# Gate projection of the first attention cut into pieces between its units

## The chip, the cores and the metric

The kernel runs on one core of one Trainium2 chip. The metric is the device time of one execution in microseconds (us), the median of several runs. The engines of the core are TensorE (PE, matrix multiplications and transposes), VectorE (DVE), ScalarE (ACT), GpSimd (POOL) and SyncE (SP, which here issues the loads of weights).

## What is computed

Two blocks over a sequence of 256 tokens with 1024 channels, all in float32. The first block has a gated mixer and then a windowed attention; the second has a retention mixer, a latent attention and, twice, a retrieval of experts. The change lies in the windowed attention of the first block. Its reference, cut to what matters:

```python
def swa_mixer(h, k_band, v_band, pos, w_in, b_q, sinks, w_out):
    z = h @ w_in
    q, g = jnp.split(z, 2, axis=-1)
    q = rotary((q + b_q).reshape(...), pos)
    scores = jnp.einsum('bnqhrd,bnkhd->bnhrqk', q, k_band) * (HEAD_DIM ** -0.5)
    scores = jnp.where(mask, scores, -jnp.inf)
    m = jnp.maximum(jnp.max(scores, axis=-1, keepdims=True), sink)
    p = jnp.exp(scores - m)
    p = p / (jnp.sum(p, axis=-1, keepdims=True) + jnp.exp(sink - m))
    o = jnp.einsum('bnhrqk,bnkhd->bnqhrd', p, v_band).reshape(b, s, B_WIDTH)
    y = o * jax.nn.silu(g)
    return y @ w_out
```

16 query heads of 64 channels share 2 key heads; queries come in two blocks of 128. The gate g isn't used before the product with V is there: it only multiplies o.

## The kernel before

**Weights.** All weights stream from HBM in slabs of 128 partitions by 2048 numbers, in one order for the whole kernel (`SLAB_STAGES`). A slab goes through a ring of two places (`ring`, loaded by SP in halves of 1024, L384). ACT rounds each half to the shorter format `w_hi` (`split_half`, L940), and POOL makes the remainder `w_lo` = ring - `w_hi` (L2010). There are four half places for each of `w_hi` and `w_lo`. A load waits until the remainder of the half that stood in its ring place is made (`split_ready`), and a rounding waits until TensorE has used the half that stood in its place (`half_done`). Every product with weights is three matmuls, hi by hi, hi by lo, lo by hi (`triple`, L433 to L435).

**Slabs of the attention.** `b_q` (4 slabs), `b_kv` (1), `b_g` (4, the gate), `b_out` (4). A gate slab has 8 chunks of the contraction and two halves of 128 output channels: 8 x 2 x 3 = 48 matmuls over 256 tokens, into one PSUM bank (`G`), which ACT empties with Silu into `B_gT` (L1033).

**Order on TensorE.** After `b_kv` all four gate slabs are multiplied (`project_cols("b_g", ...)`), then the keys (L648) and the queries (L575) are transposed; ACT and DVE copy these out. Then `attention("b", ...)` runs. It has 12 units: units 0 to 3 hold four heads each of the first query block, units 4 to 11 two heads each of the second. The order is written out by `attention_order`: "s" is a unit's scores (a mask by the identity, L664, then the products, L667), "t" the four transposes of its probabilities (L610), "v" a product with V for one query block and half of the heads (L685). Scores run three units ahead of transposes. Before, the four "v" come after the transposes of units 2, 4, 8 and 11 (`PV_AFTER`), and all share the four banks `X` in turn: a tile waits until the tile four places earlier has been read.

**The other engines in a unit.** DVE takes the maximum (`maximum`, L1460 to L1466), ACT the exponentials (L1070, L1074), DVE divides by the sum (`normalize`, L1474 to L1477), TensorE transposes, ACT copies the transposed probabilities (L1080). On DVE the order is `normalize(k)`, `maximum(k + 2)`, and at a "v" `b_gated`: the product with the gate and its splitting into `B_yh` and `B_yl` (L1643, L1417, L1418).

**After it.** `project_wide("b_out", ...)` multiplies by the output weights: two groups of two slabs, 96 matmuls over 512 columns in all. It began when all four `b_gated` were done. Then the norm of the block and the retention follow.

Of the kernel before, what the change touches and what calls it, by code (L numbers as in the profile page):

```python
# [19 lines left out]
P = 128  # L20
T = 256
NB = T // P
D = 1024
DC = D // P
W_A = 2048
RING = 2
# [7 lines left out]
HEADS_B, KVH, DH = 16, 2, 64  # L34
# [15 lines left out]


UNITS = {"b": 12, "m": 8}
PV_AFTER = {"b": [1, 3, 7, 11], "m": [1, 3, 5, 7]}
AHEAD = 3


def attention_order(name):
    n, out, values = UNITS[name], [], 0
    for k in range(min(AHEAD, n)):
        out.append(("s", k))  # L60
    for k in range(n):
        out.append(("t", k))
        while values < len(PV_AFTER[name]) and (PV_AFTER[name][values] < k or k == n - 1):
            out.append(("v", values))
            values += 1
        if k + AHEAD < n:
            out.append(("s", k + AHEAD))
    return out
# [26 lines left out]
SLAB0, N_SLABS = first_index(SLAB_STAGES)  # L95
# [37 lines left out]
def build(nc, h_kept, slabs, x_in, cols_in, rows_in, ws_in, keys_in, pos_row, pos_col, rope_in, diff_in, out):  # L133
# [4 lines left out]
    with ctx:  # L138
# [269 lines left out]
        def _(pe):  # L408
# [37 lines left out]
                                      c == 0, c == 4 * WIDE[stage] - 1)  # L446
                return last

            def project_wide(stage, src, ready=None, first=0):

                per, groups = WIDE[stage], SLABS[stage] // WIDE[stage]

                def inputs_ready(g, p, half):
                    half_ready(SLAB0[stage] + g * per + p, 0, half)
                    if ready is not None:
                        pe.wait_ge(ready, 2 * p + half + 1)

                for g in range(first, groups):
                    for b in range(NB):
                        bank_free(wide_slab(stage, g, b), 0)  # L460
                    tail = stage in TAILS and g == groups - 1
                    for p in range(per - 2 if tail else per):
                        for half in range(2):
                            inputs_ready(g, p, half)
                            wide_half(stage, g, p, half, src, range(NB)).then_inc(half_done, 1)
                    if tail:
                        for p in (per - 2, per - 1):
                            for half in range(2):
                                inputs_ready(g, p, half)
# [88 lines left out]
            def project_cols(stage, src, k):  # L558

                project(stage, src, k, False)  # L560
# [30 lines left out]
                for i in range(2):  # L591
                    x_read(pe, stage, 2 * b + i)

            def attention(name, scores, transposes, values):
                for kind, k in attention_order(name):
                    stage = f"{name}_{kind}{k}"
                    if kind == "t":
                        pe.wait_ge(sem(f"p_{name}"), k + 1)
                    if kind == "v":
                        first = PV_AFTER[name][k - 1] + 1 if k else 0  # L600
                        for u in range(first, PV_AFTER[name][k] + 1):
                            x_read(pe, f"{name}_t{u}")
                    tile = x_begin(stage, 0)
                    if kind == "s":
                        last = scores(k, tile)
                    elif kind == "v":
                        last = values(k, tile)
                    else:
                        for to, src in transposes(k):
                            last = nc.tensor.transpose(tile[:, to:to + P], src, ident[:, :])  # L610
                    last.then_inc(x_full, 1)
# [28 lines left out]
            project_wide("b_q", hT, first=1)  # L640
            x_read(pe, "b_tr")
            project_rows("b_kv", (hKV_hi, hKV_lo), DC)
            project_cols("b_g", hT, DC)
            pe.wait_ge(sem("k_rotated"), 1)
            tile = x_begin("b_ktr", 0)
            for g in range(KVH):
# [3 lines left out]
            last.then_inc(x_full, 1)  # L650
            pe.wait_ge(sem("q_rotated"), 4)
            transpose_rows("b_qtr", B_q)
            x_read(pe, "b_ktr")
            pe.wait_ge(sem("pads_zero"), 3)
            x_read(pe, "b_qtr")
# [31 lines left out]
                return last  # L687

            pe.wait_ge(sem("b_mask_ready"), 1)
            attention("b", b_scores, b_transposes, b_values)  # L690
            pe.wait_ge(sem("b_y_ready"), 4)
            project_wide("b_out", (B_yh, B_yl))


            transpose_block("r_tr", h, "h_b", 0)
# [220 lines left out]
        def _(act):  # L916
# [141 lines left out]
                        nc.scalar.activation(dst[:, :, at(n, 256)], tile[:, :].rearrange("p (b n) -> p b n", b=NB),  # L1058
                                             ACT.Copy).then_inc(free, 1)

            def attention(name, sinks, scale, round_to=None):
                for kind, k in attention_order(name):
                    stage = f"{name}_{kind}{k}"
                    if kind == "s":

                        s, row = units[name][k]
                        act.wait_ge(sem(f"max_{name}"), k + 1)
                        n = s.shape[1]
                        if sinks:
                            nc.scalar.activation(esink[:, row:row + n], esink[:, row:row + n], ACT.Exp)  # L1070
                        tile, free = x_tile(act, stage, 0)
                        for u in range(n):
                            keys = s.shape[2]
                            last = nc.scalar.activation(s[:, u, :], tile[:, u * keys:(u + 1) * keys], ACT.Exp,  # L1074
                                                        bias=negm[:, row + u:row + u + 1], scale=scale,
                                                        accum_out=rsum[:, row + u:row + u + 1])
                        last.then_inc(free, 1)
                    elif kind == "t":
                        tile, free = x_tile(act, stage, 0)
                        nc.scalar.activation(probsT[name][k], tile[:, :], ACT.Copy).then_inc(free, 1)  # L1080
                    elif round_to is not None:
                        tile, _ = x_tile(act, stage, 0)
                        nc.scalar.activation(flat(round_to[:, 2 * k:2 * k + 2, :]), tile[:, :], ACT.Copy
                                             ).then_inc(sem(f"rounded_{name}"), 1)
# [64 lines left out]
            round_block("b_tr", hKV_hi, 1, "kv_g", "rounded_kv", "b_rest")  # L1149
            only_split("b_q", 1, 3)  # L1150
            only_split("b_kv")
            take_cols("b_g", B_gT, ACT.Silu)
            tile, free = x_tile(act, "b_ktr", 0)
            act.wait_ge(sem("pads_zero"), 2)
            nc.scalar.activation(flat(B_kTe)[0:64, :], tile[0:64, :], ACT.Copy)
# [2 lines left out]
            act.dma_start(flat(R_diff), diff_in).then_inc(sem("diff_loaded"), 16)  # L1158
            row(fin_g, "fin_g", "lnw_loaded")
            take_T("b_qtr", B_qT)  # L1160
            attention("b", True, DH ** -0.5)
            seam("b_out", "fin", "r_v", lambda: round_block("r_tr", hT_hi, 0))


# [141 lines left out]
        def _(dve):  # L1306
# [145 lines left out]
                    last = V.tensor_tensor(y[:, :, :, 32:64], x2, t[1], ALU.add)  # L1452
                last.then_inc(done, 1)

            def attention(name, sinks, scale, prepare, take_values):

                def maximum(k):
                    s, row = units[name][k]
# [23 lines left out]
                for kind, k in attention_order(name):  # L1482
                    if kind == "t":
                        normalize(k)
                        if k + 2 < UNITS[name]:
                            maximum(k + 2)
                    elif kind == "v":
                        take_values(k)

# [149 lines left out]

            def b_gated(k):  # L1640
                b, i = k // 2, k % 2
                tile, free = x_tile(dve, f"b_v{k}", 0)
                V.tensor_tensor(B_yT[:, 4 * i:4 * i + 4, b * P:(b + 1) * P], tile[:, :].rearrange("p (a t) -> p a t", a=4),  # L1643
                                B_gT[:, 4 * i:4 * i + 4, b * P:(b + 1) * P], ALU.mult).then_inc(free, 1)
                x_read(dve, f"b_v{k}")
                split(*[x[:, 4 * i:4 * i + 4, b * P:(b + 1) * P] for x in (B_yh, B_yl, B_yT)]
                      ).then_inc(sem("b_y_ready"), 1)

            g_read(dve, "b_g")
            attention("b", True, DH ** -0.5, b_unit, b_gated)  # L1650
            def final_norm(tiles, b):

                inverse_root("fin", b)
# [334 lines left out]
        def _(pool):  # L1988
# [51 lines left out]
            for i, (a, part) in enumerate(((B_kTe, slice(64, P)), (B_kTo, slice(0, 64)), (B_vz, slice(0, P)))):  # L2040
                Q.memset(flat(a)[part, :], 0.0).then_inc(sem("pads_zero"), 1)
                pool.wait_ge(sem("pads_zero"), i + 1)
            split(SLAB0["b_q"] + RING, SLAB0["v0"] + RING)
            pool.wait_ge(split_ready, 2 * SLAB0["m_in"])
            split(SLAB0["m_in"], SLAB0["m_in"] + RING)
            pool.wait_ge(half_done, 2 * SLAB0["m_in"])
# [128 lines left out]
```

## Time and profile before

| | |
|---|---|
| median of 3 runs | 2396.67 us (2395.88 to 2397.43) |
| profiled execution, its time | 2396.03 us |
| profiled execution, its span | 2394.3 us |
| mean granted TensorE clock | 0.979 |
| PE busy | 2301.3 us (96%) |
| DVE busy | 1491.6 us (62%) |
| ACT busy | 1165.7 us (49%) |
| POOL busy | 1137.6 us (48%) |
| read from HBM | 394.13 MB, 166 GB/s |

A span starts with the first instruction and ends with the last; the execution's own time has 1.7 us around it. Busy times count instructions at work; a PE that is busy may be working at half clock. The granted clock is a share of full speed: 1.00 is 2.4 GHz and 0.50 is 1.2 GHz. A row of the timeline gives the start, the duration and the engine, the line, the operation and its operands, how many instructions were merged (x), and in brackets the idle time just before and what ended it. The duration of one matmul includes its way through the array, so that matmuls in a row overlap: their cost is the distance between their starts.

### The profile page before, as it was taken

The page shows a single profiled execution, that of the slowest core. Times are in us where ns is not written, and L with a number is a line of the kernel's source. Part 1 is how long each engine was busy: PE and PEld are TensorE (multiplying, and loading weights), DVE is VectorE, ACT ScalarE, POOL GpSimd, SP SyncE. Part 2 cuts the span into 40 slices and gives each one's busy share as a digit, 9 for nine tenths or more (in the row PEclk, how much of TensorE's full clock was granted, in tenths as well). Part 3 has the DMA queues.
Part 4 walks back from the last instruction along what each step waited for, and adds up shares of the span by engine and source line. Part 5 has one row for each costly group of instructions (what it writes and reads, how often), then busy time and mean ns, then how long its engine had stood idle before and what let it go on. Part 6 is the DMA issues. An engine that isn't in the chain of part 4 may idle for free. (4 is left out here: it accounts for less than half of the span.)

```text
span 2394.3 us, 42935 instructions
## 1 busy us (share of the span) xinstructions
PE 2301.3 (96%) x13868; PEld 2053.1 (86%) x13868; DVE 1491.6 (62%) x3173; ACT 1165.7 (49%) x1775; POOL 1137.6 (48%) x493
## 2 busy tenths in 40 slices
PE   7999889999999999999999988799999999999998
PEld 6997868898999999988888878699999998888886
DVE  5433442332595888877777762409858886877777
ACT  5445534353455677743333343444557776333332
POOL 6867528676788666650000043367876666100000
PEclk9999989999999999999999996999999999999999
DMA  7545415545455444455566553254554444655653
GB/s 267 171 149 167 159 44 177 166 148 186 158 180 185 154 143 144 142 192 196 193 192 210 193 161 101 64 183 157 185 167 144 144 142 166 203 192 194 210 193 130
DMA packets 109592, 398.27 MB, mean 166 GB/s; under 512 B 12752, under 2 KB 13136, under 8 KB 108752
## 3 DMA queue, kind: packets, MB, share of 16 engines
q1 hardware_dynamic: 104688, 380.16, 47.9%
q10 hardware_dynamic: 4832, 17.17, 2.1%
q8 instruction: 44, 0.72, 0.1%
q14 instruction: 28, 0.23, 0.0%
HBM read 394.13 MB, written 3.15 MB: 166 GB/s over the span
## 5 line engine op out<-in xcount | busy, mean ns | idle before, releaser
L2010 POOL TENSOR_TENSOR w_lo<-ring,w_hi 128x1024 fp32r<-128x1024 f32 x474 | 1130.3, 2410 | 903.0 <-ACT w_hi L940 902.8
L940 ACT ACTIVATE w_hi<-ring 128x1024 fp32r<-128x1024 f32 x722 | 742.6, 1056 | 545.9 <-PE XX L435 391.9
L433 PE MATMUL GG<-hT_both,w_hi 128*128 128x256 f32 x1728 | 493.1, 285 | 6.3 <-DVE hT_both L1390 4.2
L434 PE MATMUL GG<-hT_both,w_hi 128*128 128x256 f32 x1728 | 491.5, 284 | 0.0
L435 PE MATMUL GG<-hT_both,w_lo 128*128 128x256 f32 x1728 | 491.4, 284 | 0.0
L543 PE MATMUL GG<-hT_both,w_hi 128*128 128x512 f32 x1152 | 410.8, 399 | 0.1
L433 PE MATMUL XX<-w_hi,hT_both 128*128 128x512 f32 x1024 | 398.7, 389 | 2.6 <-DVE w_lo L1876 2.2
L434 PE MATMUL XX<-w_lo,hT_both 128*128 128x512 f32 x1024 | 398.4, 389 | 0.0
L435 PE MATMUL XX<-w_hi,hT_both 128*128 128x512 f32 x1024 | 398.4, 389 | 0.0
L433 PEld LDWEIGHTS GG<-hT_both,w_hi 128*128 128x128 f32 x1728 | 334.4, 193 | 8.0 <-issue 5.2
L1876 DVE TENSOR_TENSOR w_lo<-ring,w_hi 128x1024 fp32r<-128x1024 f32 x248 | 304.0, 1226 | 55.6 <-ACT w_hi L940 55.4
L434 PEld LDWEIGHTS GG<-hT_both,w_hi 128*128 128x128 f32 x1728 | 334.3, 193 | 0.3 <-issue 0.2
L435 PEld LDWEIGHTS GG<-hT_both,w_lo 128*128 128x128 f32 x1728 | 334.3, 193 | 0.0
L545 PE MATMUL GG<-hT_both,w_lo 128*128 128x256 f32 x1152 | 321.6, 279 | 0.0
L543 PEld LDWEIGHTS GG<-hT_both,w_hi 128*128 128x128 f32 x1152 | 216.3, 188 | 48.4 <-issue 0.7
L433 PEld LDWEIGHTS XX<-w_hi,hT_both 128*128 128x128 f32 x1024 | 192.2, 188 | 43.6 <-DVE w_lo L1876 3.0
L435 PEld LDWEIGHTS XX<-w_hi,hT_both 128*128 128x128 f32 x1024 | 192.2, 188 | 40.2
L434 PEld LDWEIGHTS XX<-w_lo,hT_both 128*128 128x128 f32 x1024 | 192.2, 188 | 39.7
L545 PEld LDWEIGHTS GG<-hT_both,w_lo 128*128 128x128 f32 x1152 | 217.3, 189 | 0.0
L1813 DVE TENSOR_SCALAR hot<-XX,picksT 128x128 f32<-128x128 f32 x512 | 174.1, 403 | 0.0
L1868 DVE CAST hT_both<-big 128x256 fp32r x248 | 73.0, 294 | 118.0 <-PE XX L435 117.2
L1219 ACT ACTIVATE hot<-iota,picksT 128x128 f32<-128x128 f32 x384 | 124.8, 389 | 3.9 <-issue 2.1
(292 smaller groups left out, 2740.7 us busy)
## 6 DMA issues: line engine op xcount, KB each, us to landing
ring<-slabs_in SPq DMA_DIRECT2D x722, 512.0 KB, 4.2
big<-rows_in ACTq DMA_DIRECT2D x10, 512.0 KB, 6.7
big<-rows_in ACTq DMA_DIRECT2D x3, 1024.0 KB, 9.3
big<-keys_in ACTq DMA_DIRECT2D x2, 1024.0 KB, 8.2
h_kept<-h ACTq DMA_DIRECT2D x2, 1024.0 KB, 11.1
h<-h_kept ACTq DMA_DIRECT2D x2, 1024.0 KB, 6.5
big<-ws_in ACTq DMA_DIRECT2D x1, 1024.0 KB, 15.2
out<-h SPq DMA_DIRECT2D x4, 256.0 KB, 2.0
```

What stands on the lines that cost most here:

```text
L433: nc.tensor.matmul(out, a_hi, b_hi, start=start, stop=False, skip_group_check=True)
L434: nc.tensor.matmul(out, a_hi, b_lo, start=False, stop=False, skip_group_check=True)
L435: return nc.tensor.matmul(out, a_lo, b_hi, start=False, stop=stop, skip_group_check=True)
L543: nc.tensor.matmul(bank[:, a, :], w[0], hT_both[:, c, :, :].rearrange("p s t -> p (s t)"), start=c == 0, stop=False, skip_group_check=True)
L545: last = nc.tensor.matmul(bank[:, a, 0:T], w[1], hT_hi[:, c, :], start=False, stop=c == DC - 1, skip_group_check=True)
L940: nc.scalar.activation(w_hi[:, 2 * j + half, :], ring[j][:, half * 1024:(half + 1) * 1024], ACT.Copy).then_inc(hi_ready, 1)
L1219: last = nc.scalar.activation(hot[:, 0, g, q, :], iota[:, :], ACT.Abs, bias=picksT[:, 0, bass.ds(group * 4 + q, 1)], scale=-1.0)
L1813: last = V.tensor_scalar(hot[:, 1, g, q, :], counting, picksT[:, 1, t], picksT[:, 2, t], ALU.is_equal, ALU.mult)
L1868: V.tensor_copy(hT_hi[:, j, :], x).then_inc(sem(f"gated_hi{l}"), 1)
L1876: V.tensor_tensor(w_lo[:, 2 * slot + j % 2, :], ring[slot][:, (j % 2) * 1024:(j % 2 + 1) * 1024], w_hi[:, 2 * slot + j % 2, :], ALU.subtra ...
L2010: Q.tensor_tensor(w_lo[:, 2 * j + half, :], ring[j][:, half * 1024:(half + 1) * 1024], w_hi[:, 2 * j + half, :], ALU.subtract).then_inc(sp ...
```

## The change

- The gate slab 0 is multiplied where all four were. Slabs 1 to 3 are cut into 24 pieces (`gate_chunk`: one chunk of the contraction, 6 matmuls). Four pieces come between the transposes of the queries and the first scores; two come ahead of the transposes of each of units 0 to 9, and ahead of TensorE's wait for the probabilities (`gate_chunks`).
- The products with V move: the first after the transposes of unit 10, the others (in the order 2, 1, 3) after those of unit 11.
- ACT rounds the halves of the gate's slab 3 and of the first two output slabs between units, and takes the Silu of gate slabs 1 to 3 after the copy of unit 9 (`gates_taken`). DVE instead of POOL makes the remainders of these six halves (`rest_half`), after units 2, 3, 5, 7, 9 and 11; POOL goes on with the third output slab.
- The output projection's first slab waits for the two gated products 0 and 2 (the first half of the channels in both blocks), the second slab for all four. Before, everything waited for all four.
- The order of the second attention ("m") stays as it was.

```diff
-PV_AFTER = {"b": [1, 3, 7, 11], "m": [1, 3, 5, 7]}
+VALUES_OF = {"b": [range(0, 2), range(2, 4), range(4, 8), range(8, 12)], "m": [range(2 * i, 2 * i + 2) for i in range(4)]}
+VALUES_AT = {"b": {10: [0], 11: [2, 1, 3]}, "m": {2: [0], 4: [1], 6: [2], 7: [3]}}
...
-            def project_wide(stage, src, ready=None, first=0):
+            def project_wide(stage, src, ready=None, first=0, needed=lambda p, half: 2 * p + half + 1):
...
-                        pe.wait_ge(ready, 2 * p + half + 1)
+                        pe.wait_ge(ready, needed(p, half))
...
                     if kind == "t":
+                        if between is not None:
+                            between(k)
                         pe.wait_ge(sem(f"p_{name}"), k + 1)
...
-            project_cols("b_g", hT, DC)
+            project_slab(SLAB0["b_g"], 0, hT, DC, False)
+
+            def gate_chunk(n):
+
+                s, c = SLAB0["b_g"] + 1 + n // DC, n % DC
+                half = c // 4
+                if c == 0:
+                    bank_free(s, 0)
+                q = half_ready(s, 0, half)
+                for a in range(2):
+                    last = triple(G[s % 4][:, a * T:(a + 1) * T],
+                                  [x[:, q, (c % 4) * 256 + a * P:(c % 4) * 256 + (a + 1) * P] for x in (w_hi, w_lo)],
+                                  [x[:, c, :] for x in hT], c == 0 and a == 0, c == DC - 1)
+                if c % 4 == 3:
+                    last.then_inc(half_done, 1)
+
+            def gate_chunks(k):
+
+                for n in range(4 + 2 * k, min(6 + 2 * k, 3 * DC)):
+                    gate_chunk(n)
...
             transpose_rows("b_qtr", B_q)
+            for n in range(4):
+                gate_chunk(n)
...
-            attention("b", b_scores, b_transposes, b_values)
-            pe.wait_ge(sem("b_y_ready"), 4)
-            project_wide("b_out", (B_yh, B_yl))
+            attention("b", b_scores, b_transposes, b_values, gate_chunks)
+            project_wide("b_out", (B_yh, B_yl), sem("b_y_ready"), needed=lambda p, half: 2 * p + 2)
...
-            take_cols("b_g", B_gT, ACT.Silu)
+            take_cols("b_g", B_gT, ACT.Silu, count=1)
...
-            attention("b", True, DH ** -0.5)
+            def gates_taken():
+
+                split_half(SLAB0["b_out"] + 1, 1)
+                for j in range(1, 4):
+                    tile, free = g_tile(act, "b_g", j, j)
+                    nc.scalar.activation(flat(B_gT)[:, j * 512:(j + 1) * 512], tile[:, :], ACT.Silu).then_inc(free, 1)
+
+            attention("b", True, DH ** -0.5, then={
+                0: lambda: split_half(SLAB0["b_g"] + 3, 0), 1: lambda: split_half(SLAB0["b_g"] + 3, 1),
+                3: lambda: split_half(SLAB0["b_out"], 0), 5: lambda: split_half(SLAB0["b_out"], 1),
+                7: lambda: split_half(SLAB0["b_out"] + 1, 0), 9: gates_taken})
...
+            def rest_half(s, half):
+
+                dve.wait_ge(hi_ready, 2 * s + half + 1)
+                V.tensor_tensor(w_lo[:, 2 * (s % 2) + half, :], ring[s % 2][:, half * 1024:(half + 1) * 1024],
+                                w_hi[:, 2 * (s % 2) + half, :], ALU.subtract).then_inc(split_ready, 1)
...
             def b_gated(k):
                 b, i = k // 2, k % 2
+                for s in (SLAB0["b_g"] + 2 * i, SLAB0["b_g"] + 2 * i + 1):
+                    dve.wait_ge(g_free[s % 4], tiles_before(s) + 1)
...
-            g_read(dve, "b_g")
-            attention("b", True, DH ** -0.5, b_unit, b_gated)
+            dve.wait_ge(split_ready, 2 * (SLAB0["b_g"] + 3))
+            attention("b", True, DH ** -0.5, b_unit, b_gated, {
+                2: lambda: rest_half(SLAB0["b_g"] + 3, 0), 3: lambda: rest_half(SLAB0["b_g"] + 3, 1),
+                5: lambda: rest_half(SLAB0["b_out"], 0), 7: lambda: rest_half(SLAB0["b_out"], 1),
+                9: lambda: rest_half(SLAB0["b_out"] + 1, 0), 11: lambda: rest_half(SLAB0["b_out"] + 1, 1)})
...
-            split(SLAB0["b_q"] + RING, SLAB0["v0"] + RING)
+            split(SLAB0["b_q"] + RING, SLAB0["b_g"] + 3)
+            pool.wait_ge(split_ready, 2 * (SLAB0["b_out"] + RING))
+            split(SLAB0["b_out"] + RING, SLAB0["v0"] + RING)
```

## Rows read from the trace of the kernel before

**Rows 1.** Windows: attention, output projection; busy us by engine, PEclk, DMA, GB/s.

```profile
273.80:332.70 58.90, 42.21 (x243) 35.35 (x241) 32.28 (x118) 27.31 (x96) 5.45 (x3) 0.86 0.16 54
332.70:354.50 21.80, 21.80 (x89) 17.96 (x90) 5.74 (x11) 7.67 (x9) 10.61 (x5) 0.92 0.30 97
```

**Rows 2.** Waits in 273.8:332.7: waiter, released by, us in total, times, longest.

```profile
DVE big L1643 <- PE XX L685: 16.4, 4, 8.1
PE XX L610 <- DVE big L1477: 10.1, 11, 2.1
PE GG L433 <- DVE B_yl L1418: 2.0, 1, 2.0
PE XX L575 <- ACT big L1156: 1.9, 1, 1.9
```

**Rows 3.** Timeline of PE: gate's first matmul, key and query transposes, first scores.

```profile
250.74 0.28 PE L433 MATMUL GG<-hT_both,w_hi 128*128 128x256 f32 x1
...
273.78 0.60 PE L648 MATMUL XX<-ident,big 128*128 128x128 f32 x4
...
277.60 0.68 PE L575 MATMUL XX<-ident,big 128*128 128x128 f32 x4 [1.91 <-ACT big L1156]
279.49 0.77 PE L664 MATMUL XX<-B_mask_r,ident_r 128*128 128x512 f32 x1 [1.20 <-DVE big L1423]
```

**Rows 4.** Timeline of PE: a unit's scores, the next unit's transposes and scores.

```profile
286.95 0.47 PE L664 MATMUL XX<-B_mask_r,ident_r 128*128 128x512 f32 x1
...
288.80 0.66 PE L610 MATMUL XX<-ident,big 128*128 128x128 f32 x4 [0.48 <-DVE big L1477]
289.25 0.50 PE L664 MATMUL XX<-B_mask_r,ident_r 128*128 128x512 f32 x1
```

**Rows 5.** Timeline of PE: third and last products with V, output projection's start, its successor.

```profile
312.73 3.81 PE L685 MATMUL XX<-big 128*128 128x128 f32 x32 [0.26 <-ACT big L1080]
316.30 0.48 PE L664 MATMUL XX<-B_mask_r,ident_r 128*128 128x512 f32 x1
...
324.70 6.00 PE L685 MATMUL XX<-big 128*128 128x128 f32 x32 [0.89 <-ACT big L1080]
332.68 0.79 PE L433 MATMUL GG<-w_hi,B_yh 128*128 128x512 f32 x1 [1.97 <-DVE B_yl L1418]
...
356.18 1.03 PE L586 MATMUL XX<-ident,h 128*128 128x128 f32 x8
```

**Rows 6.** Timeline of DVE: maxima of two units in a row, the last gating.

```profile
305.72 0.68 DVE L1460 TENSOR_REDUCE mx<-XX 128x2 f32<-128x512 f32 x1
...
307.70 0.69 DVE L1460 TENSOR_REDUCE mx<-XX 128x2 f32<-128x512 f32 x1
...
330.74 0.69 DVE L1643 TENSOR_TENSOR big<-XX,big 128x512 f32<-128x512 f32 x1 [8.10 <-PE XX L685]
```

**Rows 7.** The page's groups: DVE's weight remainders; busy, mean ns, idle before.

```profile
L1876 DVE TENSOR_TENSOR w_lo<-ring,w_hi 128x1024 fp32r<-128x1024 f32 x248 | 304.0, 1226 | 55.6 <-ACT w_hi L940 55.4
```

**Rows 8.** Timeline of ACT: a rounding of weights, a table load, the next activation.

```profile
345.55 1.06 ACT L940 ACTIVATE w_hi<-ring 128x1024 fp32r<-128x1024 f32 x1 [1.66 <-PE GG L435]
346.63 1.28 ACT L997 ACT_TABLE_LOAD   x1
347.93 0.20 ACT L997 ACTIVATE idle<-iota 128x1 f32<-128x1 f32 x1
```

**Rows 9.** Windows for the clock, columns as in Rows 1.

```profile
281.00:283.00 2.00, 2.00 (x10) 1.90 (x10) 0.86 (x2) 0.00 (x0) 0.00 (x0) 0.50 0.96 377
287.00:290.00 3.00, 2.52 (x18) 2.18 (x17) 2.76 (x16) 2.24 (x12) 0.00 (x0) 1.00 0.00 0
326.00:328.00 2.00, 2.00 (x11) 2.00 (x11) 0.00 (x0) 0.00 (x0) 0.00 (x0) 0.50 0.00 0
334.00:336.00 2.00, 2.00 (x6) 1.54 (x6) 0.00 (x0) 0.00 (x0) 0.00 (x0) 0.50 0.00 0
```

**Rows 10.** Timeline of POOL: its first remainder after the attention.

```profile
338.52 2.39 POOL L2010 TENSOR_TENSOR w_lo<-ring,w_hi 128x1024 fp32r<-128x1024 f32 x1 [58.26 <-ACT w_hi L940]
```

More of the change, by code:

```diff
@@ L52 @@
 UNITS = {"b": 12, "m": 8}
-PV_AFTER = {"b": [1, 3, 7, 11], "m": [1, 3, 5, 7]}
+VALUES_OF = {"b": [range(0, 2), range(2, 4), range(4, 8), range(8, 12)], "m": [range(2 * i, 2 * i + 2) for i in range(4)]}
+VALUES_AT = {"b": {10: [0], 11: [2, 1, 3]}, "m": {2: [0], 4: [1], 6: [2], 7: [3]}}
 AHEAD = 3
 def attention_order(name):
-    n, out, values = UNITS[name], [], 0
+    n, out = UNITS[name], []
     for k in range(min(AHEAD, n)):
@@ L62, in attention_order @@
         out.append(("t", k))
-        while values < len(PV_AFTER[name]) and (PV_AFTER[name][values] < k or k == n - 1):
-            out.append(("v", values))
-            values += 1
+        out += [("v", i) for i in VALUES_AT[name].get(k, [])]
         if k + AHEAD < n:
@@ L592, in block_taken, with attention @@
                     x_read(pe, stage, 2 * b + i)
-            def attention(name, scores, transposes, values):
+            def attention(name, scores, transposes, values, between=None):
                 for kind, k in attention_order(name):
@@ L597, in attention @@
                     if kind == "t":
+                        if between is not None:
+                            between(k)
                         pe.wait_ge(sem(f"p_{name}"), k + 1)
                     if kind == "v":
-                        first = PV_AFTER[name][k - 1] + 1 if k else 0
-                        for u in range(first, PV_AFTER[name][k] + 1):
+                        for u in VALUES_OF[name][k]:
                             x_read(pe, f"{name}_t{u}")
@@ L1059, in take_rows, with attention @@
                                              ACT.Copy).then_inc(free, 1)
-            def attention(name, sinks, scale, round_to=None):
+            def attention(name, sinks, scale, round_to=None, then={}):
                 for kind, k in attention_order(name):
@@ L1080, in attention @@
                         nc.scalar.activation(probsT[name][k], tile[:, :], ACT.Copy).then_inc(free, 1)
+                        if k in then:
+                            then[k]()
                     elif round_to is not None:
@@ L1453, in rotate_bank, with attention @@
                 last.then_inc(done, 1)
-            def attention(name, sinks, scale, prepare, take_values):
+            def rest_half(s, half):
+                dve.wait_ge(hi_ready, 2 * s + half + 1)
+                V.tensor_tensor(w_lo[:, 2 * (s % 2) + half, :], ring[s % 2][:, half * 1024:(half + 1) * 1024],
+                                w_hi[:, 2 * (s % 2) + half, :], ALU.subtract).then_inc(split_ready, 1)
+            def attention(name, sinks, scale, prepare, take_values, then={}):
                 def maximum(k):
@@ L1486, in attention @@
                             maximum(k + 2)
+                        if k in then:
+                            then[k]()
                     elif kind == "v":
```

## The prediction

> **What bounds the kernel now.** The page comes first: PE is busy for 96% of the span, DVE for 62%, ACT and POOL for about half. So a change can only pay where PE stands still or works at half clock. The windows by stage show such a place. In the 58.9 us from the first key transpose to the output projection PE is busy for 42.2 us, at a mean clock of 0.86, while DVE has 32.3 us of work and ACT 27.3 [rows 1]. The list of waits of this stretch tells why: PE waits 10.1 us, in 11 pieces, for the probabilities that DVE divides, 2.0 us for the last gated product and 1.9 us for the copy of the keys; DVE in turn waits 16.4 us for the four products with V [rows 2]. It is a chain from engine to engine that no engine fills. Ahead of it PE multiplies the four gate slabs without a gap: 23.04 us from 250.74 to 273.78, so 5.76 a slab, 0.12 a matmul and 0.72 for a piece of six [rows 3]. The gate is needed only at the end of the chain. What work is moved into PE's waits is gained; the reader should look for how much of it fits and what is then late.
>
> **The window that is summed.** It goes from the end of gate slab 0, 250.74 + 5.76 = 256.5, to the transposes behind the output projection at 356.18 [rows 3, 5]: 99.7 us now. Ahead of it nothing changes, and what comes after it starts from the same state, shifted.
>
> **PE's work in the new order,** at full clock:
> - Key and query transposes. They wait for ACT's copy of the keys, which stands behind one Silu and two roundings as before, since ACT also does the second rounding of slab 2 here. So 277.60 - 273.78 = 3.8 us, the wait of 1.9 in it, and 0.45 for the last four: 4.3 [rows 3].
> - 24 pieces at 0.72: 17.3. The four ahead of the scores cover the 1.2 us wait for the last query copy [rows 3], and more.
> - 12 scores. From 286.95 to 288.80 less the wait of 0.48 is 1.37 [rows 4]: 16.4.
> - 12 times four transposes at 289.25 - 288.80 = 0.45 [rows 4]: 5.4.
> - Products with V. A large one takes 316.30 - 312.73 = 3.57 [rows 5], the two small ones have half as many matmuls: 3 x 3.57 = 10.7.
> - Output projection. 356.18 - 332.68 = 23.5, of which 0.08 x 21.8 = 1.7 went to the half clock [rows 1, 5]: 21.8.
>
> Together 75.9. The old window has 99.7, so 23.8 us of waits and half clock are all there is to win.
>
> **What PE still waits for.** Within a unit it now has 1.37 + 0.45 + 1.44 = 3.26 us. DVE's unit takes 307.70 - 305.72 = 1.98 [rows 6], and with a remainder of 1.23 [rows 7] 3.21. Six units of twelve have one, so 6 x 1.23 = 7.4 us more on DVE, and even those units are as short as PE's. I lay the units out on this basis and find PE the last to be ready in units 1 to 9, with 0.2 to 2 us to spare; unit 0 costs 0.2. The cover ends with the pieces, at unit 9. From the landing of the scores of unit 11 DVE has `maximum(11)` (about 1.06, half of its unit), a remainder (1.23) and `normalize(10)` (0.92), with about 0.3 of hand-over 3.5 us; PE has two pieces and four transposes, 1.9: a wait of 1.6. Then comes the one wait that the new place of the first product with V adds: `b_gated(0)` stands ahead of `normalize(11)` on DVE. PE must wait from the end of that product for the gating, 332.68 - 330.74 = 1.9 [rows 5, 6], for `normalize(11)`, 0.9, and two hand-overs, 0.4: 3.2 us. After that the products 2, 1, 3 run in one piece; gating 0 and 2 is done while 1 and 3 are multiplied, and gating 1 and 3 under the 5.4 us of the first output slab, so that the old wait of 2.0 us [rows 2] is gone. Waits: 0.2 + 1.6 + 3.2 = 5.0.
>
> **The clock.** PE fell to half clock in the sparse stretch of transposes and first scores (0.50 at 281 to 283) and again behind the last units (0.50 at 326 to 328 and at 334 to 336), but kept 1.00 in units where it was busy 2.52 us of 3 [rows 9]. In the new order the middle is denser than that. The last product with V took 6.00 us against 3.81 for its equal at full clock [rows 5]. I take one such loss, 2.2 us, for the product behind the waits of the tail, and 1.2 us for the front, where the same wait of 1.9 stays but full work follows it (bounds: nothing, and the 2.2 us of the tail's kind). The output projection then starts at full clock. Sum: 75.9 + 5.0 + 3.4 = 84.3, a gain of **15.4 us**.
>
> **What moves on the other queues.** *ACT*: six roundings at 1.06 [rows 8] between units. ACT had 27.3 us of work in 58.9 [rows 1], so a unit costs it 2.3 at most (a twelfth, the front's copies among it), with a rounding 3.3, no more than PE's 3.26 within the error of this. The exponentials of the next unit and their copy stand behind each rounding. After unit 9 the last rounding, one table load and three Silus (about 4 us together) stand ahead of the copies of units 10 and 11. Who needs these: product 1 needs the bank of copy 10, more than 5 us later, and product 3 both; `b_gated(0)` needs only the first of the three Silus, just as its product lands. Cost nothing, with a cover of 0.1 us for the Silu and 5 for the rest; if the first is gone, its delay adds to the tail one to one. A table load here takes 1.28 us and stands 0.02 us from its neighbours: 347.93 - 346.61 = 1.32 in all [rows 8]. *A rule that speaks against the change:* the Trainium skill (ScalarE: Activation LUTs, What ACT_TABLE_LOAD costs) has a drain of about 1380 ns beside the load and about 2.66 us for each switch of set. By that page the Silu would come 1.4 us later, as would `normalize(11)`, and the gain would be 14.0; the row shows no drain, and the sum goes by the row. ACT's two other loads (difference table and norm weights, 0.5 MB each) are issued 17 us earlier, when only the halves of slab 3 load, which ACT wants some 10 us later: nothing. *SP*: loads of output slabs 2 and 3 now wait for DVE's remainders after units 5 to 11, not for POOL's. The last lands some 10 us before the first output matmul, and its place in `w_hi` comes free only after it: nothing. *POOL* waits for all six of DVE's remainders, and has stood idle for 58.3 us there [rows 10]; nothing is behind it that is wanted earlier: nothing. The row for DVE's remainder is from another stage, in which POOL is idle too.
>
> **Time.** The profiled execution took 2396.03 us around its span of 2394.3; less 15.4 it is 2380.6. The median of the runs is 0.64 above that execution, so the prediction is 2396.67 - 15.4 = **2381.3**.
>
> **Rivals.**
> 1. *All of it, with no loss of clock.* The 3.4 us are not paid: 2377.9. For it: PE's front wait is alone now. Against: the tail has 4.8 us of waits within 8, as before 324.7, where the clock fell.
> 2. *The units become DVE's.* If the hand-overs between ACT's rounding and DVE's remainder don't fit beside PE, the six remainders add straight to the chain: 7.4 us back, 2388.7. For it: those units are equal within 0.05 us. Against: six of twelve have none, and PE runs three units ahead with scores.
> 3. *Slower: the clock stays low.* The pieces leave small gaps and short bursts of different kinds; if PE is granted 1.2 GHz from 257 to 318, its 17.3 + 16.4 + 5.4 + 10.7 = 49.8 us of work grow as the product with V did, by 6.00/3.81 [rows 5]: 28.6 us more, in place of the 3.4 in the sum, so 2406.5. It decides where some 19 us are added, from two thirds of that stretch on. For it: 281 to 283, with PE all busy, was at 0.50. Against: 287 to 290 at 1.00 with less work [rows 9]. The Trainium skill (TensorE: Matmul & The Clock Gate, What's actually happening) says that the slow clock is the default and activity releases it; by it this rival needs an inactive PE, which the pieces remove.
> 4. *No change.* The pieces run, but as much is late behind them (the two late products with V and their gating, with the Silus ahead): 2392 to 2401. For it: all gating is now at the end. Against: it is covered by PE's own products.
>
> **Chances.** Forecast (2379 to 2386) 0.62; rival 1 0.12; rival 2 (2386 to 2391) 0.16; rival 3 0.05; rival 4 0.05. The range 2376.5 to 2389.5 takes in the forecast, rival 1 and most of rival 2. A measurement of this kernel can tell 0.2%, 4.8 us, from no change: faster (under 2391.9) 0.90, same 0.05, slower 0.05.
>
> **What would show it.** In the profile after: the gate's matmuls L433 to L435 in pairs of pieces between L610 and L667; PE's waits for L1477 down from 10.1 us to about 5, nearly all of it in two waits before the transposes of units 10 and 11; no wait for L1418; clock 1.00 from about 266 to 300; one more table load near 301; the first output matmul near 318 and not 332.7. Wrong would be: waits in units 3 to 9 (rival 2, DVE's order); a clock of 0.5 in the middle (rival 3); `b_gated(0)` waiting for ACT; an output projection that stops for the remainder of slab 2 or 3; or a gain here that a later stage gives back.

## The result, and the profile after

| | before | changed kernel |
|---|---|---|
| median | 2396.44 us (2395.88 to 2397.43, 4 runs) | **2381.35 us** (2380.45 to 2382.11, 4 runs) |
| ratio | | 0.9934, 95% interval 0.9922 to 0.9945 |
| profiled execution, its span | 2396.03, 2394.3 | 2380.81, 2379.1 |
| PE, DVE, ACT, POOL busy | 2301.3, 1491.6, 1165.7, 1137.6 | 2294.6, 1495.3, 1166.7, 1123.8 |

The kernel is 15.1 us faster, 0.63%, and the forecast was 2381.3. Two repeats beside other runs of before gave 0.9933 (0.9915 to 0.9951) and 0.9926 (0.9913 to 0.994). That forecast and result agree so closely is partly chance, as the sum below will show.

The timeline of PE in the changed kernel has the marks of the prediction's window: the end of gate slab 0 (L668 transposes the keys), one unit, and the end of the output projection (L585).

```profile
258.12 0.60 PE L668 MATMUL XX<-ident,big 128*128 128x128 f32 x4
...
261.94 0.66 PE L574 MATMUL XX<-ident,big 128*128 128x128 f32 x4 [1.91 <-ACT big L1179]
262.36 0.40 PE L432 MATMUL GG<-hT_both,w_hi 128*128 128x256 f32 x1
...
266.80 0.40 PE L686 MATMUL XX<-B_mask_r,ident_r 128*128 128x512 f32 x1
...
281.35 0.60 PE L610 MATMUL XX<-ident,big 128*128 128x128 f32 x4
281.70 0.48 PE L686 MATMUL XX<-B_mask_r,ident_r 128*128 128x512 f32 x1
...
282.69 0.47 PE L432 MATMUL GG<-hT_both,w_hi 128*128 128x256 f32 x1
283.00 0.28 PE L433 MATMUL GG<-hT_both,w_hi 128*128 128x256 f32 x1
...
284.31 0.60 PE L610 MATMUL XX<-ident,big 128*128 128x128 f32 x4
...
299.13 0.60 PE L610 MATMUL XX<-ident,big 128*128 128x128 f32 x4
301.16 0.66 PE L610 MATMUL XX<-ident,big 128*128 128x128 f32 x4 [1.44 <-DVE big L1516]
301.66 1.95 PE L707 MATMUL XX<-big 128*128 128x128 f32 x16
306.60 0.85 PE L610 MATMUL XX<-ident,big 128*128 128x128 f32 x4 [2.99 <-DVE big L1516]
307.24 10.57 PE L707 MATMUL XX<-big 128*128 128x128 f32 x80
317.57 0.48 PE L432 MATMUL GG<-w_hi,B_yh 128*128 128x512 f32 x1
...
339.45 1.03 PE L585 MATMUL XX<-ident,h 128*128 128x128 f32 x8
```

The window took 81.33 us (258.12 to 339.45) in place of 99.7 [rows 3, 5]. Between 281.35 and 284.31 PE goes through a unit's transposes, the scores of a later unit and two pieces, and meets the next transposes without a wait. What is left are the front's wait of 1.91 us, one of 0.62 us ahead of the transposes of unit 0, and those of 1.44 and 2.99 us ahead of the transposes of units 10 and 11. The first output matmul has none, where it had 1.97 us [rows 5].

Windows of the changed kernel, columns as in [rows 1]: attention, output projection, first pieces, some units, second product with V.

```profile
258.12:317.57 59.45, 52.49 (x387) 50.26 (x385) 37.34 (x121) 35.42 (x106) 4.68 (x2) 0.94 0.30 99
317.57:339.45 21.88, 21.88 (x99) 18.07 (x98) 8.30 (x15) 9.01 (x10) 12.29 (x6) 1.00 0.29 97
264.00:266.00 2.00, 2.00 (x12) 2.00 (x11) 0.00 (x0) 0.30 (x1) 0.63 (x1) 0.51 0.79 262
275.00:280.00 5.00, 5.00 (x36) 4.70 (x36) 4.41 (x19) 5.00 (x18) 0.00 (x0) 1.00 0.01 3
308.00:310.00 2.00, 2.00 (x11) 2.00 (x11) 0.00 (x0) 0.08 (x1) 0.00 (x0) 0.50 0.47 141
```

From these marks the three parts of the span in every profile (us; from the first mark to the second is the window, "ahead" is before it, "behind" the rest of the span; where all four gate slabs come ahead of the key transposes, 17.28 us, three slabs, are taken off the first mark):

| kernel | ahead | window | behind |
|---|---|---|---|
| before, first profile and a repeat (b0_again) | 256.5, 258.6 | 99.7, 98.0 | 2038.1, 2039.1 |
| e8_loop_cut (as before, loop cut) | 259.1 | 98.0 | 2039.5 |
| e1_values_late | 256.8 | 88.7 | 2038.5 |
| changed kernel, and again (a0, a1) | 258.1, 258.0, 256.1 | 81.3, 81.4, 81.3 | 2039.7, 2039.3, 2039.6 |
| e5_output_waits | 259.8 | 85.3 | 2038.8 |
| e2_pool_rests | 257.4 | 83.8 | 2036.3 |
| e10_values_early | 256.8 | 82.5 | 2037.9 |
| e3_values_all_last | 259.5 | 77.0 | 2037.1 |
| e6_remainder_later | 256.6 | 76.2 | 2041.0 |
| e7_keys_first | 258.1 | 74.9 | 2039.0 |
| e9_slab2_on_vector | 260.7 | 72.8 | 2041.2 |

The window repeats within 0.1 us (three profiles of the changed kernel) to 1.7 us (before). The parts that no kernel here changes move by 4.6 and 4.9 us. Only part of that is shown to be chance: profiles of one and the same kernel differ by up to 2.1 us ahead and 0.9 us behind. Whether the rest belongs to the single versions isn't settled. So what an edit does inside is read from the window, and a time of a whole run can't tell a microsecond or two.

### The profile page after: what moved, and what is told of

The parts are those of the page before. It is cut to its first block and busy times, and to the rows that moved or that the text cites. A ratio compares the mean times of both kernels' runs of the same rounds, so it can differ in the third digit from the quotient of the medians.

```text
span 2379.1 us, 42927 instructions
## 1 busy us (share of the span) xinstructions
PE 2294.6 (96%) x13868; PEld 2052.0 (86%) x13868; DVE 1495.3 (63%) x3179; ACT 1166.7 (49%) x1776; POOL 1123.8 (47%) x487
## 5 line engine op out<-in xcount | busy, mean ns | idle before, releaser
L2056 POOL TENSOR_TENSOR w_lo<-ring,w_hi 128x1024 fp32r<-128x1024 f32 x468 | 1116.5, 2411 | 901.6 <-ACT w_hi L961 901.1
L781 PE MATMUL XX<-hot 128*128 128x128 f32 x1024 | 125.1, 275 | 1.7 <-DVE hot L1859 1.7
```

What stands on the lines that cost most here:

```text
L781: last = nc.tensor.matmul(X[gate_bank(l, g)][:, q * P:(q + 1) * P], hot[:, 1, g, q, :], hot[:, 0, g, q, :], start=True, stop=True)
L2056: Q.tensor_tensor(w_lo[:, 2 * j + half, :], ring[j][:, half * 1024:(half + 1) * 1024], w_hi[:, 2 * j + half, :], ALU.subtract).then_inc(sp ...
```

## Experiments

Theories: **T**, the attention is a chain from engine to engine, PE has become its bound in units 1 to 9 through the pieces, and what is left are single waits in the tail and the front. Against it stand: PE's filling alone gains; DVE's remainders set the pace; the clock; and a cost outside the window.

**The changed kernel twice more, and before once more.** No edit. The first:

> The changed kernel once more. Its first profile took 18.4 us out of the window from the end of gate slab 0 to the transposes behind the output projection (99.7 us before, 81.3 after), but was 1.6 us later than the kernel before at that window's start and 1.5 us slower behind it. Theory: these 3.1 us are the place where half clock falls, which differs from run to run, so this run again has 81.3 us (within 1) in the window, while the two parts outside move by up to 2 us each. Rival: the change costs about 3 us outside its window each time (GpSimd's loop over slabs is cut in two, the instruction stream is another); then ahead and behind come out the same as in the first profile within 0.3 us. Time 2380 to 2383 either way.

2380.37 us; window 81.4, ahead 258.0, behind 2039.3: time and window as expected, and ahead and behind within 0.1 and 0.3 us of the first profile, about as the rival has it. Two more runs decided on that:

> The kernel before once more, for its profile. The part ahead of the window ended at 256.50 us in its first profile, but at 256.8 to 259.5 in five kernels in which nothing ahead of it differs. Theory (the place of half clock ahead moves from run to run): here it ends anywhere between 256 and 260, and the part behind the window is between 2036 and 2040 us; the window itself is 99.7 within 1. Rival (the changed kernels are late there for a reason of their own): 256.5 within 0.3 again.

2397.45 us; ahead 258.6: the kernel before can be as late there as the changed one. Its window was 98.0, 1.7 less, since its output projection began at full clock this time.

> The changed kernel beside the fastest version on the same chip: 2381 within 1.5, a window of 81.4 within 1, and the parts ahead (256.5 to 259.5) and behind (2036 to 2041) somewhere in their spread.

2379.35 us (2378.57 to 2381.12); window 81.3, ahead 256.1. So the 1.6 us ahead were not the change's. Behind, its three profiles have 2039.3 to 2039.7 and the three of before's kind 2038.1 to 2039.5: on average 0.6 us more, which is less than their spread.

**The loop of GpSimd cut, in the kernel before.**

```diff
-            split(SLAB0["b_q"] + RING, SLAB0["v0"] + RING)
+            split(SLAB0["b_q"] + RING, SLAB0["b_g"] + 3)
+            split(SLAB0["b_g"] + 3, SLAB0["b_out"] + RING)
+            split(SLAB0["b_out"] + RING, SLAB0["v0"] + RING)
```

> The kernel before, with GpSimd's loop over the slabs cut in three at the places where the change cuts it, all remainders still made by GpSimd in the same order. It measures the change's other instruction stream alone. Theory: nothing, 2396.4 within 1.5, and the part behind the window between 2036 and 2040. Rival: the cut costs the 1.5 to 3 us that the changed kernel lost outside its window: 2398 to 2399.5.

2398.01 us, ratio 1.0003 (0.9993 to 1.0013): nothing.

**Products with V late, alone.** Lines from the kernel before:

```diff
-PV_AFTER = {"b": [1, 3, 7, 11], "m": [1, 3, 5, 7]}
+VALUES_OF = {"b": [range(0, 2), range(2, 4), range(4, 8), range(8, 12)], "m": [range(2 * i, 2 * i + 2) for i in range(4)]}
+VALUES_AT = {"b": {10: [0], 11: [2, 1, 3]}, "m": {2: [0], 4: [1], 6: [2], 7: [3]}}
...
-            pe.wait_ge(sem("b_y_ready"), 4)
-            project_wide("b_out", (B_yh, B_yl))
+            project_wide("b_out", (B_yh, B_yl), sem("b_y_ready"), needed=lambda p, half: 2 * p + 2)
```

> The kernel before with one part of the change alone: products with V after units 10 and 11, the output projection's first slab waiting for two gated products. No pieces, remainders made by GpSimd as before. Theory (the chain from engine to engine is the cost, and both parts shorten it): the units run at VectorE's pace, 4 x 2.26 + 6 x 1.98 = 21 us from the first to the tenth, and the first output matmul comes about 8.6 us earlier, near 324, at full clock: 2386.5, so over half of the gain of the whole change. Rival (the filling of PE's waits by pieces is what gains): the products with V only change their place, the old waits of 10 us behind VectorE stay, and no more than the 2.0 us wait before the output projection and its 1.7 us of half clock are won: 2393.

2386.61 us, ratio 0.9962 (0.9948 to 0.9976), first output matmul at 323.59. Its waits:

```profile
DVE big L1640 <- PE XX L683: 9.9, 3, 5.7
PE XX L608 <- DVE big L1474: 8.0, 12, 2.9
```

The units run at DVE's pace, and DVE's waits for products fell from 16.4 [rows 2] to 9.9 us, PE's for divisions only from 10.1 to 8.0. In windows: 98.6 (mean of the three of before's kind), 88.7, 81.3. Moving the products gains 9.9 of 17.2 us, and the pieces, with the gating and the remainders that go with them, the other 7.4. T holds; that the filling alone gains is wrong.

**The products back at their old places, with the pieces kept.** DVE copies each product out as it lands (`b_kept`) and gates the first three behind its last remainder, since the gate is there only then.

```diff
-VALUES_AT = {"b": {10: [0], 11: [2, 1, 3]}, ...
+VALUES_AT = {"b": {2: [0], 4: [1], 8: [2], 11: [3]}, ...
...
+            def b_kept(k):
+                tile, free = x_tile(dve, f"b_v{k}", 0)
+                V.tensor_copy(b_part(B_yT, k), tile[:, :].rearrange("p (a t) -> p a t", a=4)).then_inc(free, 1)
...
-                9: lambda: rest_half(SLAB0["b_out"] + 1, 0), 11: lambda: rest_half(SLAB0["b_out"] + 1, 1)})
+                9: lambda: rest_half(SLAB0["b_out"] + 1, 0),
+                11: lambda: (rest_half(SLAB0["b_out"] + 1, 1), b_gated(0), b_gated(2), b_gated(1))})
```

> The changed kernel with the products with V back at their old places (after units 2, 4, 8 and 11); VectorE copies them out and gates three of them behind its last remainder and the fourth as it lands. Theory (with the pieces PE bounds the units, so that the place of the products costs nothing as long as no gating stands ahead of a division): a window of 77 to 79, as with all products last. Rival (VectorE's waits for the products, 16.4 us before, keep the chain as long as before): 85 or more.

Window 82.5, between the two expectations; its one execution took 2378.87 us. With the pieces, and with the gating late, the place of the products hardly matters (1.2 us), so the two parts of the change overlap: each can hide the same waits. I had left out who holds the last product:

```profile
312.13 5.52 PE L707 MATMUL XX<-big 128*128 128x128 f32 x32 [2.95 <-ACT big L1101]
```

It waits 2.95 us for ACT's copies of units 10 and 11, which stand behind the last rounding, the table load and three Silus, and then runs partly at half clock. In the changed kernel three products lie over those.

**All products last.**

```diff
-VALUES_AT = {"b": {10: [0], 11: [2, 1, 3]}, ...
+VALUES_AT = {"b": {11: [0, 2, 1, 3]}, ...
```

> The changed kernel, but the first product with V after unit 11 too, so that the transposes of unit 11 don't stand behind its gating. Theory: the wait of 3.0 us ahead of those transposes becomes about 0.8, and since PE is no longer idle for long in the tail, the half clock of 3.4 us there (1.6 us lost) goes with it or moves: the window falls from 81.3 to 77.5 to 79. Rival: the gating of the first product then falls behind the other three and the output projection waits for it: the window stays at 81.

```profile
302.57 0.66 PE L610 MATMUL XX<-ident,big 128*128 128x128 f32 x4 [1.44 <-DVE big L1516]
303.49 0.66 PE L610 MATMUL XX<-ident,big 128*128 128x128 f32 x4 [0.27 <-DVE big L1516]
303.99 10.88 PE L707 MATMUL XX<-big 128*128 128x128 f32 x96
```

Window 77.0, 2374.43 us, ratio 0.991 (0.9887 to 0.9933). The wait of 2.99 us is 0.27, and all four products run at full clock in 10.6 us. The 4.4 us are 2.7 of wait and the 1.6 us that the half clock had cost.

**The remainder after unit 9 moved behind unit 11,** on top of that:

```diff
-                9: lambda: rest_half(SLAB0["b_out"] + 1, 0), 11: lambda: rest_half(SLAB0["b_out"] + 1, 1)})
+                11: lambda: (rest_half(SLAB0["b_out"] + 1, 0), rest_half(SLAB0["b_out"] + 1, 1))})
```

> As the run with all products with V last, and the remainder that VectorE makes after unit 9 moved behind unit 11. Theory: it is the only one of the six on the path: the wait ahead of the transposes of unit 10, 1.44 us there, falls by 1.2, and the window from 77.0 to 75.8. Rival: unit 11's path is then next and takes it back: 77.0.

Window 76.2: 0.8 of the 1.2 us. The wait ahead of unit 10 is 0.30 now and that ahead of unit 11 rose from 0.27 to 0.62. Its time, 2376.96 us (2375.47 to 2378.47), isn't under that of the run before: its part behind the window was 3.9 us longer.

**The six remainders made by GpSimd.**

```diff
-            attention("b", True, DH ** -0.5, b_unit, b_gated, {
-                2: lambda: rest_half(SLAB0["b_g"] + 3, 0), ...
+            attention("b", True, DH ** -0.5, b_unit, b_gated)
...
-            split(SLAB0["b_q"] + RING, SLAB0["b_g"] + 3)
-            pool.wait_ge(split_ready, 2 * (SLAB0["b_out"] + RING))
-            split(SLAB0["b_out"] + RING, SLAB0["v0"] + RING)
+            split(SLAB0["b_q"] + RING, SLAB0["v0"] + RING)
```

> The changed kernel, but the six remainders made by GpSimd, 2.4 us each, instead of VectorE, 1.22 each. Theory: PE bounds units 1 to 9, so there VectorE's 7.3 us less change nothing; only the remainder after unit 9 is on the path (the wait ahead of the transposes of unit 10, 1.5 us in the profile), so about 1.2 us less in the window, 80.1. Rival 1: VectorE's remainders also set the pace of the units: 3 us or more less. Rival 2: GpSimd at 2.4 us is too late for slab 3 of the gate, or slows VectorE beside it: the window grows.

Window 83.8, 2.5 us longer, so rival 2 and not T. (Its one execution took 2379.26 us and isn't longer than the changed kernel's, since its part behind the window is the shortest of all, 2036.3.) The timelines of DVE and POOL show how:

```profile
275.14 3.04 DVE L1516 TENSOR_SCALAR big<-big,rden 128x128 f32<-128x128 f32 x4
278.11 0.68 DVE L1499 TENSOR_REDUCE mx<-XX 128x2 f32<-128x512 f32 x1
278.82 2.23 DVE L1503 SCALAR_TENSOR_TENSOR mx<-mx,big 128x2 f32<-128x2 f32 x1
```

```profile
275.72 2.38 POOL L2052 TENSOR_TENSOR w_lo<-ring,w_hi 128x1024 fp32r<-128x1024 f32 x1 [11.83 <-ACT w_hi L961]
278.65 2.38 POOL L2052 TENSOR_TENSOR w_lo<-ring,w_hi 128x1024 fp32r<-128x1024 f32 x1 [0.54 <-ACT w_hi L961]
```

The second instruction of DVE has two numbers per partition and takes 0.16 us elsewhere in this trace; here it takes 2.23 and ends at 281.05, as POOL's does at 281.03. The four divisions take 3.04 us in place of 0.87, to 278.18, while POOL works to 278.10. The maximum between them, which reads PSUM, keeps its 0.68. Beside two later remainders of POOL the same kind of instruction takes 0.69 and 0.70 us and ends within 0.01 us of them. So six instructions on POOL don't lighten DVE: some of DVE's stand still until POOL's is through. PE waits 0.52 and 1.14 us for it in units 2 and 3, where it waited for nothing.

The tail has a second cause. The wait in unit 10 fell from 1.44 to 0.84 us, with no remainder ahead of its division, but that in unit 11 rose from 2.99 to 4.03:

```profile
305.53 0.69 DVE L1686 TENSOR_TENSOR big<-XX,big 128x512 f32<-128x512 f32 x1 [3.67 <-ACT big L1189]
```

Here `b_gated(0)` does wait for the Silu. The product had ended at 304.35, so the gating is 1.05 us later than with the old hand-over of 0.13. The prediction had given the Silu a cover of 0.1 us and said that a delay beyond it adds to the tail one to one; in this run it did.

**Keys and queries copied ahead of ACT's roundings,** on top of the remainder moved:

```diff
-            take_cols("b_g", B_gT, ACT.Silu, count=1)
+            tile, free = g_tile(act, "b_g", 0, 0)
+            nc.scalar.activation(flat(B_gT)[:, 0:512], tile[:, :], ACT.Silu).then_inc(free, 1)
...
             take_T("b_qtr", B_qT)
+            split(SLAB0["b_g"] + RING)
```

> As the run before this one, and ScalarE copies the transposed keys and queries ahead of its two roundings of gate slab 2, not behind them. Theory: PE's wait of 1.9 us ahead of the last query transposes is gone, and if the clock fell because of that wait, the 1.6 us lost at half clock in the first four pieces too: a window of 72.3 to 73.9. Rival: the roundings, now 2 us later, are late for the pieces of slab 2 or push the first exponentials back: no gain.

Window 74.9 and 2373.44 us (2373.3 to 2373.68), ratio 0.9902 (0.9886 to 0.9919): 1.3 of the 2.3 to 3.9 us. The front wait of 1.91 us and the half clock behind it are gone together, but the roundings are late, as the rival said. Waits in the window:

```profile
DVE mx L1501 <- POOL w_lo L2058: 5.4, 1, 5.4
PE XX L610 <- DVE big L1518: 3.6, 3, 2.7
```

DVE's wait for `split_ready`, which the change has put ahead of the first maximum, holds it until POOL has made slab 2's remainders, and PE's wait ahead of the transposes of unit 0 is 2.67 us, where it was 0.61.

**These two remainders on DVE as well.**

```diff
-            dve.wait_ge(split_ready, 2 * (SLAB0["b_g"] + 3))
+            dve.wait_ge(split_ready, 2 * (SLAB0["b_g"] + 2))
+            rest_half(SLAB0["b_g"] + 2, 0)
+            rest_half(SLAB0["b_g"] + 2, 1)
...
-            split(SLAB0["b_q"] + RING, SLAB0["b_g"] + 3)
+            split(SLAB0["b_q"] + RING, SLAB0["b_g"] + 2)
```

> As the run with keys and queries copied first. There VectorE waited 5.4 us for GpSimd's remainders of gate slab 2 before its first maximum (the wait that the change had added stood behind them), and that gave back most of the front. Here VectorE makes these two remainders itself, ahead of its first maximum, at 1.22 us each. Theory: the first maximum comes 2.0 us earlier, PE's wait ahead of the transposes of unit 0 falls from 2.67 to 0.6, the window from 74.9 to 72.8: 2371.5. Rival: the first exponentials then wait for ScalarE's own roundings, and the window stays above 74.

The attention in its profile, columns as in [rows 1]:

```profile
260.74:311.61 50.87, 49.38 (x386) 47.10 (x385) 39.86 (x123) 35.37 (x106) 0.00 (x0) 1.00 0.34 115
```

Window 72.8, as expected, at full clock throughout and with PE waiting 1.5 us in all. The time, 2374.95 us (2373.75 to 2376.41), ratio 0.9904 (0.9889 to 0.992), missed the expectation of 2371.5: in this profile ahead is the longest of all, 260.7, and behind too, 2041.2. Beside it on the same chip the changed kernel took 2379.35, so the version beats both kernels; that it beats the one before it, time doesn't show. All four of its executions lie above the four of that one (2373.3 to 2373.68), which ran on another chip.

**The output projection waiting for all four.**

```diff
-            project_wide("b_out", (B_yh, B_yl), sem("b_y_ready"), needed=lambda p, half: 2 * p + 2)
+            project_wide("b_out", (B_yh, B_yl), sem("b_y_ready"), needed=lambda p, half: 4)
```

> The changed kernel, but the output projection waits for all four gated products again. Theory: the wait of 1.9 us before it is back, and the clock doesn't fall for it, since PE is dense before: a window of 83.3. Rival: it was hidden otherwise (the first output matmul isn't on the path): 81.4.

```profile
321.63 0.47 PE L432 MATMUL GG<-w_hi,B_yh 128*128 128x512 f32 x1 [2.16 <-DVE B_yl L1451]
```

```profile
323.00:325.00 2.00, 2.00 (x6) 1.58 (x5) 0.00 (x0) 0.00 (x0) 0.00 (x0) 0.50 0.00 0
```

Window 85.3, 4.0 us longer, not 1.9 (one execution, 2385.63 us). The wait is back with 2.16 us, and the clock did fall (0.50 at 323 to 325), though PE had worked for 11 us without a gap before: the projection took 345.09 - 321.63 = 23.5 us in place of 21.9.

## Why the prediction was right

**Where the time lies.** Waits on the chain and half clock, not work: confirmed. PE's busy time in the whole kernel fell by 6.7 us only, with the same 13868 matmuls; the window fell by 16.7 to 18.4. Of the 18.4 us of the first profiles at most 6.4 are clock: half clock cost up to 0.14 x 58.9 + 0.08 x 21.8 = 10.0 us before [rows 1] and 3.6 after, an upper bound, since PE stood idle for part of it. The rest lies in the waits.

**The sum, step by step.** Predicted for the window 84.3, measured 81.3.
- Key and query transposes: 4.3 said, 262.36 - 258.12 = 4.2.
- *Scores, the term that was mis-sized.* 1.37 us each said. From 281.70 to 282.69 it is 0.99 in a unit of two heads, and 1.13 in one of four: 12.4 us for twelve, not 16.4. Two things were wrong with the row of before. It ended with a wait, so that the 1.37 held the last matmul's way through the array, which the next piece now covers: 0.24 each, 2.9 us. And it was a unit of four heads, where eight of the twelve have two: 0.14 each, 1.1 us.
- Transposes: 0.45 each said. They take 0.35 in the eight units 1 to 8, and 0.41, 0.60, 0.50 and 0.64 in units 0, 9, 10 and 11, which have a wait ahead of them or behind them: 5.0 us in all, 0.4 less than the 5.4.
- Two pieces: 284.31 - 282.69 = 1.62, not 1.44. From the first matmul behind the scores to the next it is 0.31 us (282.69 to 283.00) and not 0.12; 1.7 more over ten units. These three make 2.7 us less, most of the 3.0 of the error.
- Waits: 5.0 said. Unit 0 has 0.62, unit 10 1.44, unit 11 2.99, 5.05 together, and none from units 1 to 9. `b_gated(0)` standing ahead of `normalize(11)` was the largest single cost left, and all products last took it away.
- Half clock: 3.4 said. By the granted clock it is 0.06 x 59.45 = 3.6, by distances 3.1: the first four pieces took 266.80 - 262.36 = 4.44 us for 2.88, and the products 1.95 + 317.57 - 307.24 = 12.28 for 10.7. It lies in the two places that were named, the first pieces (0.51) and the product behind the tail's waits (0.50).
- Output projection 21.8 said, 21.88 at 1.00.

**Why the total fits all the same.** In the profile the 3.0 us too much in the sum were met by 1.6 us ahead and 1.5 us behind. The repeats show the first as chance; so the close agreement of the totals is chance too. It also rests on the window before, which was, with 99.7, at the long end of 98.0 to 99.7.

**Edits costed at nothing.** The table load before the Silus took 1.28 us and stood 0.02 us from the rounding ahead, as in [rows 8], and `b_gated(0)` didn't wait for it:

```profile
300.58 1.06 ACT L961 ACTIVATE w_hi<-ring 128x1024 fp32r<-128x1024 f32 x1
301.66 1.28 ACT L1189 ACT_TABLE_LOAD   x1
302.96 1.57 ACT L1189 ACTIVATE big<-GG 128x512 f32<-128x512 f32 x3
```

The drain of the Trainium skill's page (ScalarE: Activation LUTs, What ACT_TABLE_LOAD costs) isn't there. POOL's waiting cost nothing: its first remainder behind the attention again waited for ACT's rounding, after 57.17 us idle. *Not argued*: why the remainders go to DVE. The prediction called DVE's 7.4 us cost and POOL idle, and the run with POOL showed the reason: there POOL would hold DVE up. The Trainium skill has the rule (Advanced Engine Details and Errata, VectorE Performance Modes and GPSIMD Details): GpSimd shares a port of VectorE's, and collides with those of its instructions that use two ports or have two inputs in SBUF. The trace of that run agrees: the one of 2.23 us for 0.16 has two such inputs, and the maximum over PSUM isn't touched (0.68). Also passed over was the new wait ahead of DVE's first maximum; it cost nothing here, as POOL was through at 264.6, but it was what e7 ran into.

**Rivals.** 1 (no half clock) fell, as it came behind the front's and the tail's waits. 2 (units become DVE's): no PE wait in units 1 to 9. 3: clock 1.00 in the middle. 4: no.

## What to carry to other kernels

Where a stage is a chain over several engines, look for work that is wanted only at its end, and put it ahead of the waits in small pieces. Another order can hide the same waits (here the late products), and then the two gains don't add up. After this change the next costs were single places in the queues. On the engine that feeds the bound, nothing that can itself wait should stand ahead of the work that the bound needs next: a gating ahead of a division cost 2.7 us of wait and 1.6 us of half clock, a wait for another engine's remainders 2.1 us. Take the cost of a short step from a row of the same form in which it is followed by work, not by a wait.

## What the hardware showed beyond that

- POOL's subtraction of 128x1024 holds some of DVE's instructions to its end: 2.23 us for 0.16, and 3.04 us for four divisions that take 0.87. A maximum over PSUM beside it kept its 0.68 us.
- PE fell to half clock behind one wait of 2.16 us that followed 11 us without a gap, at a cost of 1.6 us, while in the kernel before the same wait of 1.97 us was followed by half clock in one profile and by full clock in two (a repeat and e8). In the runs with all products last, waits of 0.27 to 1.44 us in the attention's tail brought none, and neither did the wait of 2.67 us ahead of unit 0 in e7 (1.00 over its whole attention).
- Equal instruction streams differ by 4.6 us in the first 260 us and by 4.9 us in the last 2040, over the profiles of all versions. The windows behind the output projection show the clock in it, here of the changed kernel and of the run with POOL's remainders:

```profile
339.45:583.50 244.05, 235.71 (x1476) 210.36 (x1475) 76.91 (x140) 105.25 (x128) 173.03 (x73) 0.97 0.50 169
```

```profile
341.22:585.30 244.08, 235.40 (x1495) 210.61 (x1494) 76.86 (x140) 107.47 (x131) 174.36 (x74) 0.99 0.51 171
```

Both begin at the same place of the program and are equally long; at a clock of 0.99 PE began 19 matmuls more in it than at 0.97. What sets the place of half clock there wasn't settled, nor whether it comes by chance or with the version.
